# Five edits in a two-layer kernel: vectors turned later, pairwise waits in the mixing, half rooms loaded ahead, one gathered tile first, last pieces regrouped

## What is computed

```
x = first_block(x, ...)        # hybrid layer: rms_norm, h @ w_in, RG-LRU, sparse attention, w_out, feed-forward
# second layer
u = rms_norm_2(x, norm1_g)
proj = u @ w_in_2              # q, k, v, hyena inputs, two gates
merged = g_attn * (attn @ w_branch_attn) + g_hyena * (hyena @ w_branch_hyena)
x = x + merged @ w_out_2
# experts: each of 16 experts takes its 32 best tokens
aff = softmax(u2 @ w_router);  g, idx = top_k(aff.T, 32)
xin = u2[idx]
eo  = (silu(xin @ w_gate[e]) * (xin @ w_up[e])) @ w_down[e]     # three 1024 x 1024 matrices per expert
x   = x + scatter(eo * g)
```

## Time and profile before

| what | value |
|---|---|
| median of 3 runs | 1182.19 us (1180.73 to 1182.23) |
| the profiled execution's own time | 1180.19 us |
| its span | 1178.4 us |
| PE, DVE, ACT, POOL busy | 94%, 43%, 36%, 1% of the span |
| chain that ended last | PE 73%, DMA 22% of the span |
| HBM read | 307.53 MB, 262 GB/s over the span |

### The profile page before, as it was taken

One profiled execution on the slowest core, in us unless ns is written; L12 is line 12 of the kernel. 1 busy time (PEld: TensorE's weight loads), 2 busy tenths in 40 slices (PEclk: granted clock), 3 DMA queues, 4 the chain that ended last, 5 costly groups with the idle time before them and its releaser, 6 DMA issues.

```text
span 1178.4 us, 16674 instructions
## 1 busy us (share of the span) xinstructions
PE 1104.6 (94%) x6707; PEld 787.2 (67%) x6707; DVE 504.6 (43%) x996; ACT 422.0 (36%) x805; POOL 16.9 (1%) x29
## 2 busy tenths in 40 slices
PE   8999999999999999999999998998978897889787
PEld 7999988888999999798678886432323232323232
DVE  4778774895767555576975523010001000100010
ACT  4667667744666444674355402000000000000000
POOL 3000000000000000000000010000000000000000
PEclk9999999999999999999999999999999999999999
DMA  8735333443455667254223786999999999999998
GB/s 234 261 133 187 125 129 124 139 147 137 150 210 151 173 179 199 87 206 152 72 88 127 278 365 238 357 428 428 429 428 427 426 428 431 428 427 428 428 423 299
DMA packets 98949, 309.46 MB, mean 263 GB/s; under 512 B 6272, under 2 KB 41352, under 8 KB 87432
## 3 DMA queue, kind: packets, MB, share of 16 engines
q1 hardware_dynamic: 98136, 307.42, 68.0%
q0 software_dynamic: 496, 1.07, 0.4%
q10 hardware_dynamic: 256, 0.10, 0.0%
HBM read 307.53 MB, written 1.05 MB: 262 GB/s over the span
## 4 chain that ended last, share of the span: by engine, by line
PE 73%; DMA 22%; DVE 2%; SPq 1%; ACT 1%; issue 1%; ACTq 0%; DVEq 0%
PE bank L444 72%; DMA ring<-in_w_up 4%; DMA arena<-in_w_up 3%; DMA parts_room<-in_w_up 3%; DMA arena<-in_w_gate 3%; DMA xh<-in_w_gate 3%; DMA parts_room<-in_w_gate 3%; DMA xh<-in_w_down 1%; DMA arena<-in_filt_w 1%; PE bank L682 0%; SPq L1128 0%; DVE parts L1768 0%; DVE roots_room L1740 0%; SPq L1154 0%; DVE hidden_parts L1981 0%
## 5 line engine op out<-in xcount | busy, mean ns | idle before, releaser
L444 PE MATMUL bank<-parts 128*128 128x256 f32 (+1 forms) x2352 | 300.0, 288 | 1.2 <-issue 1.1
L444 PEld LDWEIGHTS bank<-parts 128*128 128x128 f32 x2352 | 288.4, 191 | 15.1 <-issue 12.0
L1338 ACT ACTIVATE parts<-ring 128x512 fp32r<-128x512 f32 x328 | 203.4, 628 | 227.9 <-PE bank L444 216.6
L1768 DVE TENSOR_TENSOR parts<-ring,parts 128x512 fp32r<-128x512 f32 x328 | 218.8, 689 | 121.1 <-ACT parts L1338 119.3
L444 PE MATMUL bank<-hidden_parts,parts 128*128 128x256 f32 x1024 | 164.9, 283 | 0.0
L444 PE MATMUL bank<-arena 128*32 128x512 f32 (+5 forms) x516 | 147.4, 500 | 9.2 <-DMA arena<-in_w_down 2.7
L444 PE MATMUL bank<-arena,roots_room 128*32 128x512 f32 x400 | 129.5, 614 | 16.4 <-DMA arena<-in_w_up 4.0
L444 PEld LDWEIGHTS bank<-hidden_parts,parts 128*128 128x128 f32 x1024 | 141.4, 192 | 0.1
L2289 DVE TENSOR_TENSOR sqr<-bank,arena 128x512 f32<-128x512 f32 x8 | 5.2, 686 | 269.7 <-ACT arena L1655 269.7
L444 PEld LDWEIGHTS bank<-arena 128*128 128x128 f32 (+3 forms) x516 | 74.4, 192 | 52.6 <-issue 41.1
L444 PE MATMUL bank<-ring,roots_room 128*32 128x512 f32 x224 | 101.5, 616 | 6.8 <-DMA xh<-in_w_up 4.0
(11 more groups left out here) (308 smaller groups left out, 989.7 us busy)
## 6 DMA issues: line engine op xcount, KB each, us to landing
ring<-in_w_in SPq DMA_DIRECT2D x21, 2048.0 KB, 7.9
arena<-in_w_gate SPq DMA_DIRECT2D x13, 2048.0 KB, 35.4
arena<-in_w_down SPq DMA_DIRECT2D x12, 2048.0 KB, 36.6
arena<-in_w_up SPq DMA_DIRECT2D x10, 2048.0 KB, 38.5
ring<-in_w_ff_in SPq DMA_DIRECT2D x8, 2048.0 KB, 7.9
ring<-in_w_ff_out SPq DMA_DIRECT2D x8, 2048.0 KB, 9.0
parts_room<-in_w_up SPq DMA_DIRECT2D x8, 2048.0 KB, 36.8
ring<-in_w_gate SPq DMA_DIRECT2D x7, 2048.0 KB, 34.9
```

The source lines that it names most:

```text
L444: return nc.tensor.matmul(o, lhsT=l, rhs=r, start=first, stop=last)
L1338: A(w_part[0][:, p % PIECES], piece_of(n, p), ACT.Copy).then_inc(S("pieces rounded"), 1)
L1768: X.tensor_tensor(w_part[1][:, p % PIECES], piece_of(n, p), w_part[0][:, p % PIECES].bitcast(F32), ALU.subtract).then_inc(S("pieces split" ...
```

## The change

Five edits, in the order of the program.

1. PE does job (0, 1) ahead of `turn_vectors` and `filter_layer(0)`. The second vectors go to bank 5 in place of bank 7. DVE does `rest_of_half(0)` ahead of the copies of the vectors.
2. In the mixing the one wait for four adds becomes four waits, one ahead of every second k of the first job's first tile.
3. The last two of the ten rooms (units 8 and 9) are loaded in halves: their upper halves (rows 2 and 3) right after unit 6, with no wait of their own, their lower halves where the whole rooms were loaded.
4. Ahead of the first products only gathered tiles 0 (bank 6) and 1 (bank 5) are made. Tiles 2 and 3 are made after row 0's products, and row 1 waits for DVE to have taken tiles 1, 2 and 3.
5. Of the last four units, rows 0 and 1 are loaded whole (1024 columns, 2 MB each) and used for both column halves; rows 2 and 3 stay in column halves, first both of h = 0, then both of h = 1. So two units' four transfers become two.

```diff
@@ start, TensorE
-            pe.wait_ge(S("tables loaded"), 16)
-            turn_vectors(0, ROWS_A)
-            turn_vectors(1, ROWS_B)
-            filter_layer(0)
             slot_ready(0)
             dense_bank((0, 1))
             for t in range(TT):
                 last = token_major(0, 1, t, hT, 256, 512)
             dense_done(last, (0, 1))
+            pe.wait_ge(S("tables loaded"), 16)
+            turn_vectors(0, ROWS_A)
+            turn_vectors(1, ROWS_B)
+            filter_layer(0)
@@ start, VectorE
             for k in range(KD):
                 wait_taken(("h", k // 2))
                 rest_of_h(hT, 0, k)
+            rest_of_half(0)
             dve.wait_ge(S("vectors 0 turned"), 1)
...
             filter_argument(0)
-            rest_of_half(0)
             rate()
@@ mixing
-            pe.wait_ge(S("merged2"), 4)
...
+                        if j == 0 and t == 0 and k % 2 == 0:
+                            pe.wait_ge(S("merged2"), k // 2 + 1)
                         last = mm(ps[:, t * T:t * T + T], w[:, k, c:c + P], merged2[:, k, :], k == 0, k == KD - 1)
@@ first gathered tile
+            take(6, ("gathered", 6))
+            take(5, ("gathered", 5))
+            gather_first(6, 0).then_inc(S("gathered"), 1)
+            gather_first(5, 1)
...
                     for j in range(RUN):
-                        if j == 2:
+                        if j == 1:
+                            gather_first(5, 2)
+                            gather_first(5, 3).then_inc(S("rest gathered"), 1)
                             wait_taken(("gathered", 5))
@@ last pieces, TensorE
+                if last_group:
+                    for j in range(2):
+                        for h in range(2):
+                            last_pieces(h, (j,))
                 for h in range(2):
                     if last_group:
-                        last_pieces(h)
+                        last_pieces(h, (2, 3))
@@ loads, SyncE
+                if n == MOE_RING - 3:
+                    for late in upper_first:
+                        load_rows_of(late, 2, RUN)
+                if n in upper_first:
+                    sp.wait_ge(S(free[n][0]), free[n][1])
+                    load_rows_of(n, 0, 2)
+                    continue
...
+                    if n < LAST_ROWS + 2:
+                        sp.dma_start(moe_room[n % MOE_RING].rearrange("p (e c) -> p e c", c=D), rows_of[:, n - LAST_ROWS])\
+                            .then_inc(moe_loaded[n % MOE_RING], 16)
+                        continue
+                    for j in (2, 3):
+                        h = n - LAST_ROWS - 2
+                        sp.dma_start(last_piece(h, j), rows_of[:, j, :, 512 * h:512 * h + 512])\
+                            .then_inc(S("last piece but one loaded") if h and j == 2 else moe_loaded[n % MOE_RING], 16)
```

More of the change, by code:

```diff
@@ L989, in _, with gather_first @@
             pe.wait_ge(S("picked"), 2)
[L990 to L995, removed]
+            def gather_first(b, k):
+                for t in range(TT):
+                    last = mm(bank[b][:, k * P:k * P + P], un[:, t, spaced(k)], pick[:, t, 0:P], t == 0, t == 1)
+                return last
+            take(6, ("gathered", 6))
+            take(5, ("gathered", 5))
+            gather_first(6, 0).then_inc(S("gathered"), 1)
+            gather_first(5, 1)
             ug = list(use)
@@ L1084, in experts, with last_pieces @@
                         block(2 * KD + RUN * q, (2, 3), 4, hhT, q, "lower half summed" if q else "")
-                def last_pieces(h):
-                    for j in range(RUN):
-                        n = LAST_ROWS + (RUN * h + j) // 2
+                def last_pieces(h, rows):
+                    for j in rows:
+                        n = LAST_ROWS + (j if j < 2 else 2 + h)
                         if h == 1 and j == 2:
@@ L1181, in _, with load_rows_of @@
                     ("logits", 1)]
+            upper_first = (MOE_RING - 2, MOE_RING - 1)
+            def load_rows_of(n, first, to):
+                v, e = n // (2 * RUN), n % RUN
+                rows_of = I[("w_gate_2", "w_up_2")[(n // RUN) % 2]][0, e, P * RUN * v:P * RUN * (v + 1), :]
+                sp.dma_start(moe_slot(n)[:, 0, first:to, :], rows_of.rearrange("(p j) c -> p j c", j=RUN)[:, first:to, :])\
+                    .then_inc(moe_loaded[n % MOE_RING] if first == 0 else S("upper rows loaded"), 16)
             def refill_by_rows():
@@ L1209, in _ @@
                     rows_of = I[key][0, g * GROUP:(g + 1) * GROUP, D - P * RUN:, :].rearrange("e (p j) c -> p j e c", j=RUN)
-                    for i in (2 * (n - LAST_ROWS), 2 * (n - LAST_ROWS) + 1):
-                        h, j = i // RUN, i % RUN
-                        sp.dma_start(last_piece(i), rows_of[:, j, :, 512 * h:512 * h + 512])\
-                            .then_inc(S("last piece but one loaded") if i == 2 * RUN - 2 else moe_loaded[n % MOE_RING], 16)
+                    if n < LAST_ROWS + 2:
[6 more added lines that the diff above has]
+                            .then_inc(S("last piece but one loaded") if h and j == 2 else moe_loaded[n % MOE_RING], 16)
                     continue
@@ L1708, in rest_of_h, with rest_of_piece, rest_of_half, rest_of_next @@
                     .then_inc(S("h split"), 1)
+            def rest_of_piece(i, p, first, start):
+                n = first + p // UNIT_PIECES
+                dve.wait_ge(S("pieces rounded"), i * 16 + (start + p + 1))
+                X.tensor_tensor(w_part[1][:, p % PIECES], piece_of(n, p), w_part[0][:, p % PIECES].bitcast(F32),
+                                ALU.subtract).then_inc(S("pieces split"), 1)
+            def rest_of_half(s):
+                n, h = split_halves[s]
+                for p in range(HALF_PIECES * h, HALF_PIECES * (h + 1)):
+                    rest_of_piece(0, p, n, first_piece[(n, 0)])
+            def rest_of_next(pieces, first, start):
+                for p in range(pieces):
+                    rest_of_piece(0, p, first, start)
             for k in range(KD):
@@ L1762, in filter_argument @@
                 X.tensor_scalar(t, t, 3.1415925, -3.1415925, ALU.min, ALU.max).then_inc(S("filter argument"), 1)
-            def rest_of_piece(i, p, first, start):
-                n = first + p // UNIT_PIECES
-                dve.wait_ge(S("pieces rounded"), i * 16 + (start + p + 1))
-                X.tensor_tensor(w_part[1][:, p % PIECES], piece_of(n, p), w_part[0][:, p % PIECES].bitcast(F32),
-                                ALU.subtract).then_inc(S("pieces split"), 1)
-            def rest_of_half(s):
-                n, h = split_halves[s]
-                for p in range(HALF_PIECES * h, HALF_PIECES * (h + 1)):
-                    rest_of_piece(0, p, n, first_piece[(n, 0)])
-            def rest_of_next(pieces, first, start):
-                for p in range(pieces):
-                    rest_of_piece(0, p, first, start)
             dve.wait_ge(S("vectors 1 turned"), 1)
```

31 lines of the change are left out of this document (16 added, 15 removed).

## The result

The change takes **1185.01 us** in the median (1182.22 to 1187.84, 14 runs); before, on the same chip, takes 1182.26 (1180.73 to 1184.52, 14 runs). The ratio is **1.0025, 95% interval 1.0016 to 1.0033**: slower by some 3 us. The profiled execution took 1185.18, its span is 1183.4, and the mean granted clock 0.984.

A forecast was written before the change was run, and what follows sets the result against it. PE was taken to bound the kernel up to the experts, then the weight stream and PE's work behind its last piece; 2.1 + 1.3 - 1.7 - 1.3 - 0.5 + 1.2 + 1.3 = +2.4 on 1182.19 gave 1184.6 us, range 1180.7 to 1186.7.

The forecast's parts named there:

- Start, the wait: At `dense_split(1, 1)`: DVE's new order brings its pieces later, so PE stands idle and starts late; +2.1 us.
- (b): Rival, start: PE doesn't wait for DVE's list at `dense_split(1, 1)` and keeps its 2.4 us; 1178.8 us, chance 0.08.
- ACT's root hangs on the sine: Start: the sine comes after 32.4 us, the root at about 35.8, so DVE's 0.83 us wait for it is absorbed.
- Start, the clock: Behind PE's idle time ahead of `dense_split(1, 1)` the clock falls for some 3 us; +1.3 us, bounds 0 and +1.45.
- Mixing: At the first job of the mixing: split waits remove PE's 1.7 us hole; -1.7 us, bounds -1.5 and -1.7.
- First tile: Where the experts begin: fewer tiles gathered first let the first refill go out earlier; -1.3 us, bounds -0.9 and -1.95.
- Upper halves: Loads of the last rooms: 2 MB moved ahead only leave the stream idle longer; 0, bounds 0 and -0.3 us.
- End, stream: Last loads: 4 KB rows flow at 403 GB/s where 2 KB rows had 386; -0.5 us, bounds 0 and -0.8.
- End, PE: Last pieces: more of PE's work stands behind the last transfers, so the last piece starts late; +1.2 us, bounds +0.9 and +1.45.
- End, the clock: A 3.5 us PE gap near the end drops the clock, 2.6 us of matmuls at half speed; +1.3, bounds 0 and +1.7.
- (a): Rival: the clock holds in one or both of the new gaps, at start and end; 1183.3 or 1182.0 us, chance 0.32.
- (c): Rival, experts: the stream runs dry behind row 0 and the first tile's gain is lost; 1185.9 us, chance 0.10.

The follow-up runs named there:

- e4: The change with DVE's `rate()` moved from ahead of the second half of pieces to behind the fourth; 1186.26 us, ratio 1.0027 to before.
- e2: The change with the last four units' loads and products put back as before; 1181.90 us, ratio 1.0001 to before.
- e5: The change with three idle matmuls on PE behind rows 0 and 1 of the last pieces; 1183.09 us, ratio 1.0011 to before.
- e1: The change with the start's new order undone on PE and DVE; 1182.89 us, ratio 1.0007 to before.
- e3: Before with only the mixing's split waits, upper halves loaded ahead and fewer gathered tiles first; 1179.68 us, ratio 0.9983 to before.
- e13: Before with idle matmuls on PE in the start's gap from 18.0 to 21.1 us; 1181.76 us, ratio 0.9997 to before.
- e6: Before with the mixing's split waits alone; 1180.82 us, ratio 0.9992 to before.
- e7: Before with the mixing's split waits and fewer gathered tiles first, upper halves not loaded ahead; 1180.34 us, ratio 0.9986 to before.
- e12: e9 with the end of e5 (the change's end loads plus three idle matmuls); 1177.95 us, ratio 0.9965 to before.
- e9: The change with the old end, DVE's filter argument and `rate()` later, ACT's exponential and first sine behind the second root; 1177.05 us, ratio 0.9958 to before.
- e11: e3 with PE's new order at the start and DVE's old one; 1181.81 us, ratio 0.9998 to before.
- e10: e9 with unit 2's load issued only when unit 1 has landed; 1176.56 us, ratio 0.9954 to before.

## Why the prediction was right, point by point

The forecast was 1184.6, the time is 1185.01. The sum was +2.4, measured is +3.0 (1.9 to 3.9). By its own line of 0.2% the change is slower (0.25%, interval 0.16 to 0.33), where it put 0.38 against 0.50 for no difference. The terms, by its own steps:

- **Start, the wait** (+2.1): right in kind for the place that it names: +2.46 at `dense_split(1, 1)`, behind DVE's pieces, with `rate()` starting at 32.84 in place of 29.61. That the size fits as well is in part luck. Unit 1's rounding starts 0.90 later than before, which it did not foresee, and DVE's own steps from the end of `rest_of_half(0)` to `rate()` took 3.40 us (29.44 to 32.84) where it had 3.85; from the rounding on, the new order costs 1.56. PE's lead was 1.7 us (41.51 - 4.17 = 37.34 against 39.05) and not 2.4, so rival (b) had its price too high. The step "ACT's root hangs on the sine" was right, and e4 shows that it is a second chain of the same length, not one that is absorbed.
- **Start, the clock** (+1.3): 1.47 in the profile (7.48 against 6.01, at a clock of 0.50); 1.3 in e2 and e5, 2.2 in e4.
- **What the start is worth in the median**: forecast 3.4, measured 2.1 to 2.2 (the change against e1, e2 against e3). The step that failed is the last one, in which the sum is made in the terms of one profile and the median "stands 2.0 above it". That distance isn't a constant of the kernel. It is made, in part at least, of falls of the clock, among them the one in the gap of 18.0 to 21.1, and that gap is what edit 1 closes. e13 puts it at 1.5, give or take 1: 3.9 - 1.5 = 2.4.
- **Mixing** (-1.7): 1.98 in the profiles of the change and of e6, -0.9 (-2.0 to +0.1) by itself.
- **First tile** (-1.3): the refill goes out 4.81 behind the start of the gathering and not 5.89, -1.08. As forecast, row 0 fell partly into the low stretch (0.84 in 740 to 745). This distance is 4.0 to 5.7 us in eleven profiles with the edit and 5.9 to 7.1 in three without it (before, e6, e13), so before's profile is at the fast end of its kind and the edit gives rather more than 1.08.
- **Upper halves** (0): 0.3 us in e7 against e3, not told from 0.
- **End, stream** (-0.5): 403 GB/s where before has 386, as forecast, and no version shows the gain by itself. From the first refill to the wait behind which 2 MB are still to come it is 424.0 to 425.2 us in five profiles with the new loads and 424.2 to 425.8 in four with the old ones. The Trainium skill, in DMA: Bandwidth & Descriptors, Specifications, has no such difference above 512 B; by that rule these two rates would be one, and the trace does not agree.
- **End, PE** (+1.2): 1.4 in e5's profile, 1.2 in its median against e2, 0.9 in e12 against e9.
- **End, the clock** (+1.3, bounds 0 and +1.7): this term was mis-sized, in the profile by more than any other; it measures 2.9 in the profile and 1.6 to 1.9 in the medians. I let the low stretch last for 2.6 us of matmuls. It lasted for some 7: in 1169 to 1176 the clock is 0.56 in the mean, twice as long as behind the gap at the start. It also left out that the old end could hide a fall of the clock in its waits for DMA and the new one can't.

The terms measured in medians: start +2.1, middle -2.0, end +2.8, together +2.9. The forecast had them at +3.4, -3.0 and +2.0. So the total is right by its mechanisms, and helped by errors that cancel. Of the rivals, (a) may be what the fastest executions of the change are (1182.22), though none of them was profiled, but not its median, (b) was true of nothing but a version that cuts ACT's and DVE's chain as well (e9), (c) did not occur: from 745 to 760 DMA moves 395 GB/s, and no less than 356 in any 2 us of it.

TensorE: Matmul & The Clock Gate of the Trainium skill says in its section What's actually happening that the number of slow matmuls at the start of one and the same kernel varies from run to run. The traces here are of a gap inside a kernel, and there they agree: the clock fell in two of five profiles of one and the same start.

## What to carry to other kernels

When an engine is given work in its gap, look for the chain on the other engines that ends where the gap's next wait is: if both arrive together today, filling the gap turns into idle time at the next wait, and the reorder pays only once that chain is cut too (here +2.1 us in the medians with edit 1, -3.0 with e9's start, of which 1.1 is lead). A profile is one draw: where the runs of a kernel lie in groups, find out which gap makes them before a difference of medians is put down to an edit. When transfers are regrouped, ask what the waits between them hid: here a fall of the clock cost 0 to 0.6 us in the old end and 2.9 in the new one. And a gap in which TensorE waits for a known transfer is worth some idle matmuls, if what follows hangs on its clock (-1.7 us at the end here; at the start a spread of 1.5 in place of 4, but hardly a gain, as the added work itself cost 1.2).

## What the runs showed of the hardware

- The clock falls in one and the same gap in some executions only: at the start in the profiles with a pause of 3.57 and 3.94 us, not in those with 2.78 to 3.05. The price was 1.7 us (8.86 against 7.17), and a kernel's times lie in groups about 2 us apart.
- A low stretch isn't of one length. Behind the gap of 4.17 us at the start the clock is 0.50 from 42 to 45 us and 0.95 in the next window; at the end of the change it is 0.56 over 7 us. Nor does the place settle it: behind the start's gap e4 has some 7 us (39.3 to 46.1, 0.5 throughout), behind the old end's gap e9, e11 and e13 have some 3 us, e7 and e10 some 7. What makes one twice as long isn't settled.
- A change of ACT's tables took 1.28 us and the next activation started right behind it (29.14 + 1.28, and 30.44 for the exponential). ScalarE: Activation LUTs of the Trainium skill, What ACT_TABLE_LOAD costs, gives that figure and about as much again for a drain; no such pause stands in these rows.
- ACT's first rounding, which waits for unit 1, starts 0.5 to 1.6 us later in the eight profiles in which PE reads unit 0 without a pause than in five of the six others. It is not the next load's issue (e10); the cause stays open.
